# First attention of two layers: maxima, tables and the first scores in another order

## The chip, the cores and the metric

The kernel runs on one core of one Trainium2 chip. The metric is the device time of one execution in microseconds. Before the change the median of three runs is 3340.94 us (3340.58 to 3341.14).

The core has five engines with a queue each: TensorE (PE: products; its weight loads are shown as PEld), VectorE (DVE), ScalarE (ACT), GpSimd (POOL) and SyncE (SP, DMAs only). Semaphores are what they wait for each other by.

## The reference

Two model blocks of two layers each work on 512 tokens of width 1024, in float32. Only the first block is touched by the change. Cut to what matters, its layer is:

```python
h = rmsnorm(x, g_mix)
aq, ak, av, rq, rk, rv, rg, ga, gb = jnp.split(h @ w_in, SPLIT_POINTS, axis=-1)
aq, ak = rope_half(aq, pos), rope_half(ak, pos)
ya = sliding_window_sink_attention(aq, ak, av, sinks) @ w_a   # 8 heads, window 128
...                                                           # retention: yb
mixed = jax.nn.sigmoid(ga) * ya + jax.nn.sigmoid(gb) * yb
x = x + mixed @ w_out
x = x + jnp.square(jax.nn.relu(rmsnorm(x, g_mlp) @ w_up)) @ w_down
```

The attention takes the scores of 128 queries against up to 256 keys, adds a mask, takes the row maximum (with the sink), the exponential, the sum, divides, and multiplies by the values.

## The kernel before

**Tiling.** Activations lie transposed: 8 tiles of 128 features by 512 tokens. Each float32 product is split in three: high by high, high by low, low by high, each a PE product of 128x512 (`L526` to `L528`, or `L531`, `L532`, `L583` where a panel is taken row by row). Weights come as panels of 128x2048. SP loads a panel, ACT writes its high part (`L1257`), POOL the low part by a subtraction (`L357`, `L349`), and PE multiplies: a panel of two output tiles is 48 products, and half a tile is 12.

**The start of a layer of the first block.** `L667` are warm-up products on a constant tile, before the first panel (the program's first PE work). Then PE takes panel `q` (two head pairs) and panel `kv` (keys, values) on x times the gain, not yet normalised. ACT squares x, and DVE adds the squares (`L1961`). Behind four rows of `kv` PE adds over the features (`L660`, `token_sums`), ACT takes the root (`L1537`), DVE the inverse, and PE spreads it over the partitions (`L715`, `spread`). DVE multiplies the rotary tables by it (`L2283`), so that the rotation of q and k also normalises them. Then DVE scales x again and splits it into high and low parts (`L2010`, `L1939`, ACT's high part `L1277`) for the panels that need it normalised: panel `rq` is the fourth and the first of these.

**Rotation and first attention.** A rotation (`rope`) of one 128x512 tile is four DVE instructions: a shuffle and three elementwise ones (`L1944` to `L1950`). Head pairs 0 to 3 are rotated as 0, 1, 2, 3 and the keys as 4; layer 0 takes 0 before the scaling and 4, 1, 2, 3 behind it, layer 1 takes 0, 1, 4 before it and 2, 3 behind it. The attention then runs in 8 steps of two head pairs: PE's scores (`L746`; step 0 needs rotations 1 and 4, step 1 needs rotation 3, and each step the maxima of the one before, which free its bank), DVE's maxima (`L2055`, with the sink at `L2060`), ACT's exponentials (`L1311`), DVE's division, PE's transposes (`L754`), ACT's read of them (`L1321`), PE's outputs (`L766`) and their read (`L1326`). Between these, PE takes half tiles of other panels as fillers, 32 pieces in each layer.

**What sets the order.** It is written by hand, one list for each engine, and a wait names the mark of another engine's instruction. Each engine keeps its own order strictly. In layer 0 PE takes two filler pieces (one tile) ahead of scores 0, and ACT reads that tile and issues the second table's DMA before its first exponentials. The table of the second rotation (retention, `ROT`) may be loaded only once rotation 3 has used the first.

Of the kernel before, what the change touches and what calls it, by code (L numbers as in the profile page):

```python
# [191 lines left out]
SWAP_A = [r ^ 16 for r in range(32)]  # L192
# [34 lines left out]
def program(nc, stream, x_in, consts_in, rot_in, vec_in, wgate_in, pos_in, out, marks):  # L227
    ctx = ExitStack()
    with ctx:
# [282 lines left out]
        def _(pe):  # L512
# [150 lines left out]
            def start_clock(n):  # L663

                T.after("warm_tile", own=False)
                for _ in range(n):
                    pe.matmul(PS[:, 7, 0:2 * P], TMP[:, 3, 0:P], TMP[:, 3, 0:2 * P], start=True, stop=True)  # L667
# [300 lines left out]
                    marks[("panel", end - 2)] = ("up_full", base_t + 4 * groups - 2)  # L968
                marks[(t, l, "ffn_out")] = ("down_added", done)

            start_clock(5)
            for l in range(DEPTH):
                w, t = at_a(l), "a"
                h_ready = lambda k: (t, l, "h_lo", k)
# [6 lines left out]
                    run(keys, 4)  # L981
                token_sums(TMP[:, 2, :], 4, (t, l, "n1_acc", KD - 1), (t, l, "n1_ms"))
                bank_reader[4] = (t, l, "n1_root")
                run(keys, 2)
                spread(5, (t, l, "n1_inverse"), (t, l, "n1_spread"))
                bank_reader[5] = (t, l, "n1_scaled", KD - 1)
                for _ in keys:
# [19 lines left out]
                        yield from gemm_tiles(w["ga"] + p, KD, 2, XH, XL, h_ready, lambda m: (t, l, "ga", 2 * p + m), True)  # L1007
                    yield from tok_tiles(w["rv0"], h_ready, lambda m: (t, l, "rv", 0, m), True)

                attention(pairs_a(l), l, t, fillers(), 2 if l == 0 else 0)  # L1010
                for p in range(2):
                    if p:
                        gemm(w["wa"] + p, 4, 4, YH, YL, lambda k: (t, l, "ao_lo", k), lambda m: (t, l, "wa", 4 * p + m))
# [227 lines left out]
        def _(act):  # L1241
# [52 lines left out]
                e = 96 if eps == EPS else 97  # L1294
                A.done(act.activation(TMP[:, 3, :], sums, ACT.Sqrt, scale=1.0 / n, bias=ST[:, e:e + 1]), *name)

            def attention(pairs, l, t, fillers):
                steps = steps_of(pairs, t)
                last = len(steps) - 1

                def exponentials(i):
                    n, nk, c = len(steps[i]), steps[i][0]["nk"], 32 + 16 * (i % 2)
                    pr = probs(i, n * nk)
                    A.after((t, l, "negmax", i))
                    for u in range(n):
                        for v in range(2):
                            if u or v:
                                A.after()
                            e = pr[:, v, u * nk:(u + 1) * nk]
                            h = c + 2 * u + v  # L1310
                            A.done(act.activation(e, e, ACT.Exp, bias=ST[:, h + 4:h + 5],  # L1311
                                                  scale=-1.0, accum_out=ST[:, h + 8:h + 9]), t, l, "exp", i)
                    if steps[i][0]["sink"] is not None:
                        A.after()
                        sinks = ST[:, c + 12:c + 12 + 2 * n]
                        A.done(act.activation(sinks, sinks, ACT.Exp), t, l, "exp", i)

                def read_transposes(i):
                    w = len(steps[i]) * steps[i][0]["nk"]
                    A.after((t, l, "pt", i), (t, l, "o", i - 2) if i >= 2 else None)  # L1320
                    A.done(act.activation(probs_t(i, w), PS[:, 6:8, 0:w], ACT.Copy), t, l, "pt_read", i)  # L1321

                def read_outputs(i):
                    n = len(steps[i])
                    A.after((t, l, "o", i))
                    A.done(act.activation(steps[i][0]["o"](n), PS[:, 2, 0:n * P].rearrange("p (u s) -> p u s", u=n), ACT.Copy),  # L1326
                           t, l, "o_read", i)

                exponentials(0)
                exponentials(1)  # L1330
                run(fillers, tiles_in(t, -1))
                done = 0
                for i in range(last + 2):
                    if i <= last:
                        read_transposes(i)
                    if i:
                        read_outputs(i - 1)
                    if i + 2 <= last:
                        exponentials(i + 2)
                    if i <= last:  # L1340
                        run(fillers, tiles_in(t, i))
                    if i and steps[i - 1][0]["part"] == NB - 1:
                        for j in range(done, done + len(steps[i - 1])):
                            split_hi(YH[:, j, :], (AR[:, 14 + j, :] if t == "a" else AR[:, 8 + j, :]), [], (t, l, "ao_hi", j))
                        done += len(steps[i - 1])
                marks[(t, l, "pt_read")] = marks[(t, l, "pt_read", last)]
                for _ in fillers:
                    pass
# [244 lines left out]
            for l in range(DEPTH):  # L1593
# [45 lines left out]
                hi(w["rq"] + 2)  # L1639
                fill = filler_reads()  # L1640
                if l == 0:
                    run(fill)
                    const_dma(act, VEC[:, 1, :], vec_in[1], "vec1")
                A.after((t, l, "roped", 3))
                const_dma(act, ROT[:, :, :], rot_in[1], ("rot", l, 1))
                attention(pairs_a(l), l, t, fill)
                hi(w["wa"] + 1)
                if l + 1 < DEPTH:
                    A.after((t, l, "roped", 12))
# [280 lines left out]
        def _(dve):  # L1930
# [107 lines left out]
                        j = k - 1  # L2038
                        lo(XL[:, j, :], dst(j), XH[:, j, :], [hi_name(j)], lo_name(j), own=False)

            def attention(pairs, l, t, beside):
                steps = steps_of(pairs, t)
                last = len(steps) - 1

                def maxima(i):
                    n, nk, c = len(steps[i]), steps[i][0]["nk"], 32 + 16 * (i % 2)
                    pr = probs(i, n * nk)
                    sink = steps[i][0]["sink"]
                    V.after((t, l, "s", i), (t, l, "pt", i - 3) if i >= 3 else None, (t, l, "mask", steps[i][0]["part"]))
                    for u, U in enumerate(steps[i]):  # L2050
                        for v in range(2):
                            h = 2 * u + v
                            least = ST[:, 16 + sink + h:17 + sink + h] if sink is not None else -TAKEN
                            e = slice(u * nk, (u + 1) * nk)
                            V.done(dve.tensor_tensor_reduce(pr[:, v, e], U["mask"], PS[:, 4 + v, e], -(HD ** -0.5), least,  # L2055
                                                            ALU.add, ALU.min, ST[:, c + 4 + h:c + 5 + h]), t, l, "s_read", i)
                    marks[(t, l, "negmax", i)] = ("dve", V.n)
                    if sink is not None:
                        V.after()
                        V.done(dve.tensor_tensor(ST[:, c + 12:c + 12 + 2 * n], ST[:, c + 4:c + 4 + 2 * n],  # L2060
                                                 ST[:, 16 + sink:16 + sink + 2 * n], ALU.subtract), t, l, "negmax", i)

                def normalise(i):
                    n, nk, c = len(steps[i]), steps[i][0]["nk"], 32 + 16 * (i % 2)
                    pr = probs(i, n * nk)
                    V.after((t, l, "exp", i))
                    sums = ST[:, c + 8:c + 8 + 2 * n]
                    if steps[i][0]["sink"] is not None:
                        V.done(dve.tensor_tensor(sums, sums, ST[:, c + 12:c + 12 + 2 * n], ALU.add))
                        V.after()  # L2070
                    V.done(dve.reciprocal(ST[:, c:c + 2 * n], sums))
                    V.after()
                    if n == 1:
                        V.done(dve.tensor_tensor(pr, pr, ST[:, c:c + 2].unsqueeze(2).broadcast_to([P, 2, nk]), ALU.mult),
                               t, l, "p", i)
                    else:
                        for v in range(2):
                            e = pr[:, v, :].rearrange("p (u n) -> p u n", u=n)
                            V.done(dve.tensor_tensor(e, e, ST[:, c + v:c + 2 * n:2].unsqueeze(2).broadcast_to([P, n, nk]),
                                                     ALU.mult), t, l, "p", i)  # L2080

                maxima(0)
                maxima(1)
                for i in range(last + 1):
                    if t == "b":
                        run(beside, rounds(t, i))
                    normalise(i)
                    if i + 2 <= last:
                        maxima(i + 2)
                    if t == "a":  # L2090
                        run(beside, rounds(t, i))
                marks[(t, l, "s_read")], marks[(t, l, "negmax")] = marks[(t, l, "s_read", last)], marks[(t, l, "negmax", last)]
                for j in range(4):
                    lo(YL[:, j, :], AR[:, 14 + j, :] if t == "a" else AR[:, 8 + j, :], YH[:, j, :],
                       [(t, l, "ao_hi", j)], (t, l, "ao_lo", j))
# [175 lines left out]
            for l in range(DEPTH):  # L2271
# [13 lines left out]
                for j in early:  # L2285
                    rope(AR[:, j, :], SWAP_A, (t, l, "roped", j), [("read", t, l, "q", j)])
                scale_again(t, l, VA["g_mix"])
                for j in [j for j in (4, 1, 2, 3) if j not in early]:
                    rope(AR[:, j, :], SWAP_A, (t, l, "roped", j), [("read", t, l, "q", j)])

                def retention_ropes():
                    for j in range(8):
# [1 line left out]
                             YSCR[:, KD + 7, :])  # L2294
                        yield

                attention(pairs_a(l), l, t, retention_ropes())
                branch_gate(l, t)
                def per_chunk(c0):
                    return CT[:, c0:c0 + P].unsqueeze(1).broadcast_to([P, NB, P])  # L2300
# [257 lines left out]
```

How the kernel before makes its waits and increments, by code:

```python
    def after(self, *names, own=True):  # L205
        need = {}
        for name in names:
            if name is None or (name not in self.marks and not self.marks.get("complete")):
                continue
            who, n = self.marks[name]
            need[who] = max(need.get(who, 0), n)
        if own:
            need[self.name] = self.n
        for who, n in need.items():
            if n > 0:
                self.eng.wait_ge(self.sems[who], n)
# [65 lines left out]
        def const_dma(eng, dst, src, name):  # L283
            if n_consts[0]:
                eng.wait_ge(const_loaded, 16 * n_consts[0])
            eng.dma_start(dst, src).then_inc(const_loaded, 16)
            n_consts[0] += 1
            marks[name] = ("const", 16 * n_consts[0])
# [27 lines left out]
        @block.sync  # L317
# [6 lines left out]
            sp.dma_start(RAW[:, 1, :], stream[1:2, :, :].rearrange("o p n -> p (o n)")).then_inc(raw_full[1], 16)
            with sp.Fori(1, NPANELS // 2) as i:
                for s in range(2):
                    sp.wait_ge(lo_ready, 2 * i + s + 1)
                    sp.dma_start(RAW[:, s, :], stream[bass.ds(2 * i + s, 1), :, :].rearrange("o p n -> p (o n)"))\
                        .then_inc(raw_full[s], 16)
            for k in range(KD):
                sp.wait_ge(sems["act"], marks.get(("b", DEPTH - 1, "ln2_x", k), ("act", 1))[1])
                sp.dma_start(out.rearrange("(k p) s -> p k s", p=P)[:, k, :], X[:, k, :]).then_inc(stored, 16)
            sp.wait_ge(stored, 16 * KD)
```

## Time and profile before

| | us |
|---|---|
| median of the runs | 3340.94 |
| the profiled execution | 3339.35 |
| its span | 3337.5 |
| PE busy | 3301.5 (99%) |
| DVE busy | 1567.9 (47%) |
| ACT busy | 1370.2 (41%) |
| POOL busy | 1470.4 (44%) |
| waits of PE on the maxima before scores (`L746`) | 5.0, two times |
| waits of PE on ACT's first high part (`L531`) | 2.9, once |

Busy time is the time in which an engine has an instruction under way; since matmuls overlap, a busy PE may still run at half speed, which the busy share doesn't tell. The length of a product and the granted clock tell it. What PE waits for is named by the last semaphore that came.

### The profile page before, as it was taken

The numbers are of one execution on the slowest core, as the hardware profiler recorded it, in microseconds if no ns is written. First come the engines' busy times: TensorE is split into PE (matmuls) and PEld (weight loads), VectorE is DVE, ScalarE is ACT, GpSimd is POOL, SyncE is SP. The second block draws the span as 40 slices with busy tenths as digits, with TensorE's granted clock in tenths as the row PEclk, the third lists the DMA queues.
The fourth block names the chain that finished last, engine by engine and source line by source line (L and its number), as shares of the span: only waits on it lengthen the run. The fifth ranks groups of instructions, "written<-read, shape, count | busy, mean of one in ns | idle before, by whom it ended". The sixth has DMA issues, their size and how long they took to land. (4 is left out here: it accounts for less than half of the span.)

```text
span 3337.5 us, 45362 instructions
## 1 busy us (share of the span) xinstructions
PE 3301.5 (99%) x16670; PEld 2748.5 (82%) x16670; DVE 1567.9 (47%) x2488; ACT 1370.2 (41%) x1989; POOL 1470.4 (44%) x1102
## 2 busy tenths in 40 slices
PE   9999999999999999999999999999999999999998
PEld 7888888888788888888878888888887788888887
DVE  7523332226514442224973446544488625464445
ACT  5535332224635342223364453333343635443333
POOL 4433544445343444445433345445544233445453
PEclk9999999999999999999999999999999999999999
DMA  4222222222222322222211222222222121222221
GB/s 153 89 73 86 89 103 95 94 101 95 77 76 76 103 100 100 89 101 106 88 66 66 73 92 99 84 95 101 101 81 87 64 76 68 97 85 92 101 98 66
DMA packets 44014, 299.02 MB, mean 90 GB/s; under 512 B 4816, under 2 KB 5456, under 8 KB 8784
## 3 DMA queue, kind: packets, MB, share of 16 engines
q1 hardware_dynamic: 41696, 291.52, 24.5%
q10 hardware_dynamic: 2160, 5.33, 0.5%
q8 instruction: 107, 1.75, 0.2%
q14 instruction: 51, 0.42, 0.0%
HBM read 294.74 MB, written 2.10 MB: 89 GB/s over the span
## 5 line engine op out<-in xcount | busy, mean ns | idle before, releaser
L349 POOL TENSOR_TENSOR w_lo<-w_raw,w_hi 128x512 fp32r<-128x512 f32 x1024 | 1364.6, 1365 | 1778.2 <-ACT w_hi L1257 1778.2
L526 PE MATMUL ps<-x_hi,w_hi 128*128 128x512 f32 x2296 | 907.2, 395 | 3.1 <-DVE arena L2195 2.2
L528 PE MATMUL ps<-x_hi,w_lo 128*128 128x512 f32 x2296 | 894.8, 390 | 0.0
L527 PE MATMUL ps<-x_lo,w_hi 128*128 128x512 f32 x2296 | 894.1, 389 | 0.0
L1257 ACT ACTIVATE w_hi<-w_raw 128x1024 fp32r<-128x1024 f32 x516 | 515.9, 1049 | 463.0 <-PE ps L528 339.4
L526 PEld LDWEIGHTS ps<-x_hi,w_hi 128*128 128x128 f32 x2296 | 431.5, 188 | 100.3 <-issue 6.4
L528 PEld LDWEIGHTS ps<-x_hi,w_lo 128*128 128x128 f32 x2296 | 431.2, 188 | 91.2
L527 PEld LDWEIGHTS ps<-x_lo,w_hi 128*128 128x128 f32 x2296 | 431.6, 188 | 89.0 <-issue 2.2
L526 PE MATMUL ps<-y_hi,w_hi 128*128 128x512 f32 x1056 | 411.9, 390 | 2.2 <-issue 1.9
L528 PE MATMUL ps<-y_hi,w_lo 128*128 128x512 f32 x1056 | 410.9, 389 | 0.0
L527 PE MATMUL ps<-y_lo,w_hi 128*128 128x512 f32 x1056 | 410.8, 389 | 0.0
L2236 DVE TENSOR_TENSOR x<-x,ps 128x512 f32<-128x512 f32 x272 | 182.2, 684 | 255.5 <-PE ps L528 255.3
L2195 DVE SCALAR_TENSOR_TENSOR arena<-ps,vec,arena 128x511 f32<-128x511 f32 (+1 forms) x176 | 131.5, 749 | 300.4 <-ACT arena L1467 290.1
L526 PEld LDWEIGHTS ps<-y_hi,w_hi 128*128 128x128 f32 x1056 | 198.2, 188 | 45.1 <-issue 4.2
L527 PEld LDWEIGHTS ps<-y_lo,w_hi 128*128 128x128 f32 x1056 | 198.2, 188 | 41.5 <-issue 0.5
L528 PEld LDWEIGHTS ps<-y_hi,w_lo 128*128 128x128 f32 x1056 | 198.2, 188 | 41.3
L632 PE MATMUL ps<-w_hi,x_hi 128*128 128x256 f32 x768 | 222.2, 289 | 1.2 <-POOL w_lo L349 1.2
L633 PE MATMUL ps<-w_hi,x_lo 128*128 128x256 f32 x768 | 217.1, 283 | 0.0
L634 PE MATMUL ps<-w_lo,x_hi 128*128 128x256 f32 x768 | 217.1, 283 | 0.0
L1273 ACT ACTIVATE arena<-ps 128x512 f32<-128x512 f32 x136 | 81.3, 598 | 315.8 <-PE ps L528 240.6
L1467 ACT ACTIVATE arena<-ps,vec 128x512 f32<-128x512 f32 x88 | 68.4, 779 | 277.4 <-PE ps L528 277.4
L2206 DVE SCALAR_TENSOR_TENSOR arena<-ps,tmp 128x512 f32<-128x512 f32 x64 | 44.0, 691 | 238.5 <-PE ps L528 224.9
(269 smaller groups left out, 4178.7 us busy)
## 6 DMA issues: line engine op xcount, KB each, us to landing
w_raw<-stream SPq DMA_DIRECT2D x274, 1024.0 KB, 4.8
x<-x_t SPq DMA_DIRECT2D x4, 512.0 KB, 8.1
rotary<-rot ACTq DMA_DIRECT2D x4, 512.0 KB, 4.0
y_t<-x SPq DMA_DIRECT2D x8, 256.0 KB, 2.1
ct<-consts ACTq DMA_DIRECT2D x2, 770.0 KB, 4.4
arena<-pos ACTq DMA_DIRECT2D x2, 256.0 KB, 2.6
w_gate<-w_gate_in ACTq DMA_DIRECT2D x2, 256.0 KB, 2.8
vec<-vectors ACTq DMA_DIRECT2D x4, 116.0 KB, 2.0
```

The lines of the kernel that those rows point to most:

```text
L349: ins = nc.gpsimd.tensor_tensor(low(c)[:, o:o + S], RAW[:, c % 2, o:o + S], high(c)[:, o:o + S].bitcast(F32), ALU.subtract)
L526: pe.matmul(ps, wh, xh, start=(k == 0), stop=False)
L527: pe.matmul(ps, wh, xl, start=False, stop=False)
L528: return pe.matmul(ps, wl, xh, start=False, stop=last)
L632: pe.matmul(ps, xh, wh, start=(k == 0), stop=False)
L633: pe.matmul(ps, xl, wh, start=False, stop=False)
L634: mm = pe.matmul(ps, xh, wl, start=False, stop=(k == KD - 1))
L1257: act.activation(wh[:, o:o + 2 * S], RAW[:, s, o:o + 2 * S], ACT.Copy)\
L1273: A.done(act.activation(dst, bank_of(*name), func, **kw), *(("read",) + name))
L1467: act.activation(AR[:, j, :], PS[:, j, :], ACT.Identity, scale=VEC[:, l % 2, bass.ds(tap, 1)], bias=VEC[:, l % 2, bass.ds(bias, 1)]).then_ ...
L2195: ins = dve.scalar_tensor_tensor(AR[:, j, tap:S], PS[:, j, 0:n], wv, AR[:, j, tap:S], ALU.mult, ALU.add)
L2236: dve.tensor_tensor(X[:, m, :], X[:, m, :], PS[:, 4 + m % 4, :], ALU.add).then_inc(down_added, 1)
```

## The change

It moves instructions and adds three warm-up products. In words:

- PE warms up with eight products in place of five.
- The spread of the inverse root comes behind one more row of the `kv` panel, not two.
- In layer 0, PE asks for scores 0 directly behind the fourth panel (`rq`); the tile that ran ahead is now among the later fillers.
- ACT issues the DMA of the second rotary table behind exponentials 0, and in layer 0 reads one tile later.
- DVE takes maxima 0 before rotations 2 and 3, and maxima 1 behind them, in both layers.

```diff
-            start_clock(5)
+            start_clock(8)
...
-                run(keys, 2)
+                run(keys)
                 spread(5, (t, l, "n1_inverse"), (t, l, "n1_spread"))
...
-                attention(pairs_a(l), l, t, fillers(), 2 if l == 0 else 0)
+                attention(pairs_a(l), l, t, fillers())
...  ACT
                 exponentials(0)
+                for _ in behind_first:
+                    pass
                 exponentials(1)
...
                 if l == 0:
-                    run(fill)
                     const_dma(act, VEC[:, 1, :], vec_in[1], "vec1")
-                A.after((t, l, "roped", 3))
-                const_dma(act, ROT[:, :, :], rot_in[1], ("rot", l, 1))
-                attention(pairs_a(l), l, t, fill)
+
+                def second_table():
+                    A.after((t, l, "roped", 3))
+                    const_dma(act, ROT[:, :, :], rot_in[1], ("rot", l, 1))
+                    yield
+
+                attention(pairs_a(l), l, t, fill, second_table())
...  DVE
                 maxima(0)
+                for _ in behind_first:
+                    pass
                 maxima(1)
...
-                for j in [j for j in (4, 1, 2, 3) if j not in early]:
+                for j in [j for j in (4, 1) if j not in early]:
                     rope(AR[:, j, :], SWAP_A, (t, l, "roped", j), [("read", t, l, "q", j)])
+
+                def last_ropes():
+                    for j in (2, 3):
+                        rope(AR[:, j, :], SWAP_A, (t, l, "roped", j), [("read", t, l, "q", j)])
+                        yield
...
-                attention(pairs_a(l), l, t, retention_ropes())
+                attention(pairs_a(l), l, t, retention_ropes(), last_ropes())
```

On PE, in layer 0, at the end of the fourth panel (`L532` and `L583` are its last row; `arena` under `L746` holds the rotated queries and keys), before:

```order
162 L531 MATMUL ps<-x_hi,w_hi 128x512
163 L532 MATMUL ps<-x_hi,w_lo 128x512
164 L583 MATMUL ps<-x_lo,w_hi 128x512 x2
165 L526 MATMUL ps<-x_hi,w_hi 128x512
166 L527 MATMUL ps<-x_lo,w_hi 128x512
```

and now:

```order
162 L531 MATMUL ps<-x_hi,w_hi 128x512
163 L532 MATMUL ps<-x_hi,w_lo 128x512
164 L583 MATMUL ps<-x_lo,w_hi 128x512 x2
165 L746 MATMUL ps<-arena 128x128 x4
166 L526 MATMUL ps<-x_hi,w_hi 128x512
```

Scores 0 stood behind 24 filler products, at row 189, and stand ahead of them now. Scores 1 follow behind 12 products in both.

On DVE, in layer 0, behind rotations 4 and 1 (a rotation is the shuffle and three rows; `ISA` are the maxima, the second row of each pair reading out the minimum), before:

```order
40 L1944 STREAM_SHUFFLE tmp<-arena 128x512
41 L1946 TENSOR_TENSOR tmp<-tmp,rotary 128x512
42 L1948 TENSOR_TENSOR arena<-arena,rotary 128x512
43 L1950 TENSOR_TENSOR arena<-arena,tmp 128x512
44 L2055 ISA tmp,stats<-ct,ps,stats 128x128
45 L2055 ISA stats 128x1
```

and now:

```order
42 L2060 ISA tmp,stats<-ct,ps,stats 128x128
43 L2060 ISA stats 128x1
44 L2065 TENSOR_TENSOR stats<-stats 128x4
45 L1949 STREAM_SHUFFLE tmp<-arena 128x512
46 L1951 TENSOR_TENSOR tmp<-tmp,rotary 128x512
47 L1953 TENSOR_TENSOR arena<-arena,rotary 128x512
```

Rows 36 to 43 were rotations 2 and 3, with maxima 0 behind them in rows 44 to 52; now maxima 0 are rows 36 to 44 and the rotations rows 45 to 52. The same swap stands in layer 1. (Lines behind the diff's additions are five higher in the changed kernel.)

On ACT, in layer 0, around the first exponentials (`L1311`), before:

```order
22 L1257 ACTIVATE w_hi<-w_raw 128x1024 x2
23 L1273 ACTIVATE arena<-ps 128x512
24 L287 DMA vec<-vectors 128x232
25 L287 DMA rotary<-rot 128x1024
26 L1311 ACT_TABLE_LOAD
27 L1311 ACTIVATE tmp,stats<-tmp,stats 128x128 x4
```

and now:

```order
22 L1257 ACTIVATE w_hi<-w_raw 128x1024 x2
23 L287 DMA vec<-vectors 128x232
24 L1311 ACT_TABLE_LOAD
25 L1311 ACTIVATE tmp,stats<-tmp,stats 128x128 x4
26 L1316 ACTIVATE stats<-stats 128x4
27 L287 DMA rotary<-rot 128x1024
```

The read of the first filler tile (`L1273`) has gone behind exponentials 1, and the DMA of the table stands between exponentials 0 and 1.

## Rows read from the trace of the kernel before

**Rows 1.** The page, busy time, share and instructions of each engine.
```profile
PE 3301.5 (99%) x16670; PEld 2748.5 (82%) x16670; DVE 1567.9 (47%) x2488; ACT 1370.2 (41%) x1989; POOL 1470.4 (44%) x1102
```

**Rows 2.** Timeline of the start: begin, length, engine, line, tiles, [idle before].
```profile
1.35 4.64 PE L667 MATMUL ps<-tmp 128*128 128x256 f32 x10 [1.35 <-DVE tmp L1935]
...
8.91 0.77 PE L531 MATMUL ps<-x_hi,w_hi 128*128 128x512 f32 x1 [2.92 <-ACT x_hi L1566]
...
14.15 0.39 PE L531 MATMUL ps<-x_hi,w_hi 128*128 128x512 f32 x1
```

**Rows 3.** Timeline, sums of squares, token sums and spread of layer 0.
```profile
19.84 8.35 DVE L1961 TENSOR_TENSOR tmp<-tmp,scratch 128x512 f32<-128x512 f32 x6
...
28.25 1.05 PE L660 MATMUL ps<-ct,tmp 128*128 128x1 f32 x8 [0.29 <-DVE tmp L1961]
...
32.02 1.05 PE L715 MATMUL ps<-ct,stats 128*128 128x128 f32 x8
```

**Rows 4.** Timeline of ACT, the read of the keys and the first split.
```profile
35.65 1.29 ACT L1273 ACTIVATE arena<-ps 128x512 f32<-128x512 f32 x2 [6.04 <-PE ps L583]
...
38.73 1.14 ACT L1277 ACTIVATE x_hi<-tmp 128x512 fp32r<-128x512 f32 x2
```

**Rows 5.** Timeline of DVE, layer 0, splits, rotations 1 to 3, maxima 0.
```profile
39.38 1.68 DVE L1939 TENSOR_TENSOR x_lo<-tmp,x_hi 128x512 fp32r<-128x512 f32 x1 [0.38 <-ACT x_hi L1277]
...
58.75 0.69 DVE L1950 TENSOR_TENSOR arena<-arena,tmp 128x512 f32<-128x512 f32 x1
...
62.06 1.66 DVE L1948 TENSOR_TENSOR arena<-arena,rotary 128x512 f32<-128x512 f32 x1
...
67.87 0.69 DVE L1950 TENSOR_TENSOR arena<-arena,tmp 128x512 f32<-128x512 f32 x1
...
69.94 0.16 DVE L2060 TENSOR_TENSOR stats<-stats 128x4 f32<-128x4 f32 x1
```

**Rows 6.** Timeline of PE, layer 0, fourth panel's end to scores 2.
```profile
57.45 0.61 PE L583 MATMUL ps<-x_lo,w_hi 128*128 128x512 f32 x2
...
63.43 0.71 PE L746 MATMUL ps<-arena 64*128 64x128 f32 x8
...
66.70 0.39 PE L528 MATMUL ps<-x_hi,w_lo 128*128 128x512 f32 x1
70.05 0.81 PE L746 MATMUL ps<-arena 64*128 64x128 f32 x8 [2.95 <-DVE stats L2055]
...
73.72 1.13 PE L746 MATMUL ps<-arena 64*128 64x256 f32 x8
```

**Rows 7.** Timeline of POOL, its run behind the fourth panel in each layer.
```profile
60.18 6.38 POOL L349 TENSOR_TENSOR w_lo<-w_raw,w_hi 128x512 fp32r<-128x512 f32 x4 [5.06 <-ACT w_hi L1257]
...
829.47 5.62 POOL L349 TENSOR_TENSOR w_lo<-w_raw,w_hi 128x512 fp32r<-128x512 f32 x4 [3.26 <-ACT w_hi L1257]
```

**Rows 8.** Timeline of PE, layer 1, scores 0, 1 and 2.
```profile
827.27 0.71 PE L746 MATMUL ps<-arena 64*128 64x128 f32 x8
832.99 1.12 PE L746 MATMUL ps<-arena 64*128 64x128 f32 x8 [2.06 <-DVE stats L2055]
838.24 1.14 PE L746 MATMUL ps<-arena 64*128 64x256 f32 x8
```

**Rows 9.** Timeline of DVE, layer 1, rotation 2's start, 3's end, maxima 0.
```profile
823.49 0.75 DVE L1944 STREAM_SHUFFLE tmp<-arena 128x512 f32<-128x512 f32 x1
...
829.84 1.67 DVE L1950 TENSOR_TENSOR arena<-arena,tmp 128x512 f32<-128x512 f32 x1
...
832.88 1.00 DVE L2060 TENSOR_TENSOR stats<-stats 128x4 f32<-128x4 f32 x1
```

**Rows 10.** Stretch, its length, busy time by engine, granted PE clock, DMA.
```profile
833.00:837.00 4.00, 4.00 (x16) 3.17 (x17) 2.87 (x13) 3.09 (x13) 2.09 (x2) 0.57 0.50 156
```

**Rows 11.** Timeline of PE, the `wa` panel's start in layers 0 and 1.
```profile
173.56 0.47 PE L531 MATMUL ps<-y_hi,w_hi 128*128 128x512 f32 x1 [1.77 <-ACT arena L1326]
...
942.81 0.47 PE L531 MATMUL ps<-y_hi,w_hi 128*128 128x512 f32 x1 [0.84 <-ACT scratch L1273]
```

More of the change, by code:

```diff
@@ L1295, in root, with attention @@
                 A.done(act.activation(TMP[:, 3, :], sums, ACT.Sqrt, scale=1.0 / n, bias=ST[:, e:e + 1]), *name)
-            def attention(pairs, l, t, fillers):
+            def attention(pairs, l, t, fillers, behind_first=iter(())):
                 steps = steps_of(pairs, t)
@@ L2039, in norm, with attention @@
                         lo(XL[:, j, :], dst(j), XH[:, j, :], [hi_name(j)], lo_name(j), own=False)
-            def attention(pairs, l, t, beside):
+            def attention(pairs, l, t, beside, behind_first=iter(())):
                 steps = steps_of(pairs, t)
```

## The prediction

> **What bounds the kernel now.** I read the page's busy shares first, then the timeline of TensorE (PE) around each place that the diff touches, then the other engines at the same times, then the granted clock. PE is busy 3301.5 us of the 3337.5 [rows 1], so every microsecond in which PE waits or runs at half speed is a microsecond of the end, and a microsecond on another engine counts only if PE waits for it. The question is therefore where PE waits in the changed stretches, and what ends each wait.
>
> Three stretches matter. **The start**: warm-up products until 5.99, an idle 2.92 us, then the first panel from 8.91. The reader is to see that 128x512 products last 0.63 to 0.77 us here and 0.39 from 14.15 on [rows 2]: twelve products from 8.91 to 14.15 take 5.24 us, where twelve at the later pace of 0.227 us from start to start take 2.7. That is TensorE at 1.2 and then at 2.4 GHz. **First attention of layer 0**: PE sits idle 2.95 us before the second scores, at 70.05, behind VectorE's (DVE's) rotations and first maxima [rows 5, 6]. **The same place in layer 1**: 2.06 us idle before 832.99 [rows 8, 9].
>
> **Warm-up of eight products in place of five.** Five took 4.64 us, so three more take at most 2.8 and end at about 8.8, before the first panel's product at 8.91, which waits for data: they cost nothing. They may let that panel run at full speed, 2.5 us sooner. But the next thing that PE needs is the sum of squares: DVE adds until 28.19 (19.84 plus 8.35), and PE starts the token sums at 28.25, having waited 0.29 us for it already [rows 3]. DVE's chain doesn't depend on PE there. So the 2.5 us turn into a wait at the token sums of about 2.7 us, and the gain is 0. The bounds are -2.5 (carried through) and +1.6 to +1.7 (the new wait brings the clock down, see below); I take 0, since the row shows the next wait standing.
>
> **Spread one row sooner.** Its eight instructions move ahead of one row of six products, 1.4 us. DVE then scales the tables and rotates head pair 0 that much sooner. In layer 0 its next link is the first split: ScalarE (ACT) makes the high part at 38.73, right behind its weight halves, which wait for PE's keys read at 35.65 [rows 4], and DVE's first low part follows at 39.38 [rows 5]. The keys panel ends at the same time, since the spread only changed places inside it. In layer 1 rotation 4 needs the same read. Cost 0, bounds -1.4 and 0 per layer; 0, for the same reason as above.
>
> **Layer 0: the order around the first scores.** In the changed kernel PE asks for scores 0 at 57.90, right behind the fourth panel [rows 6] (57.45 plus two products), but they need rotation 1, which ends at 59.44 [rows 5]. With 0.15 us for the hand-over they run 59.6 to 60.3. DVE, free at 59.44, waits for them, then takes the maxima: 1.5 us in the calm (68.56 to 70.10) [rows 5], 2.4 us while GpSimd (POOL) subtracts (831.51 to 833.88) [rows 9]. POOL is at work from 60.18 to 66.56 [rows 7], so 2.4: until 62.7. Only now come rotations 2 and 3. One elementwise step of a rotation takes 0.69 us in the calm and 1.66 beside POOL (58.75 and 62.06) [rows 5], the shuffle 0.75 either way, so a rotation takes 3.0 or 5.9 us. Rotation 2: shuffle to 63.5, two slow steps to 66.9, one fast to 67.6; rotation 3 to 70.7; scores 1 start at 70.85. Before they started at 70.05. So removing the maxima from behind the rotations gains nothing: DVE has idled 0.9 us for the scores and pays for the maxima ahead of the rotations instead of behind them.
>
> Meanwhile PE has lost its cover. Before, it computed a whole tile (24 products) before scores 0, from 57.90 to 63.43 or 5.5 us, and half a tile behind them. Now only the half is left: PE idles 57.9 to 59.6, works to 63.1, and idles about 7.7 us until 70.85. The tile is still owed. Loss: 0.8 + 5.5 = 6.3 us. Bounds: +3.5 (all rotations calm, below) and +7.2 (one more slow step).
>
> The tile comes back at the end of attention, where the fillers of layer 0 had run out: PE idled 1.77 us before the `wa` panel. Layer 1, which never ran ahead, idled 0.84 there [rows 11]. Layer 0 now has layer 1's order: -0.9.
>
> **Layer 1.** Rotations 0, 1 and 4 stand early, so PE starts scores 0 at 827.27 in both kernels. Before, DVE went straight from the splits into rotation 2 at 823.49 [rows 9]. Now it waits from there to 828.0 with nothing to do: 4.5 us thrown away. Maxima in the calm to 829.5; POOL works from 829.47 to 835.09 [rows 7], so rotation 2 takes 5.9, to 835.4, and rotation 3 takes 3.0, to 838.4; scores 1 at 838.6 against 832.99 [rows 8]. Loss: 5.6 us; bounds +2.8 (calm) and +6.6.
>
> **The clock.** The 2.06 us idle of layer 1 was followed by a granted clock of 0.57 over 833 to 837 [rows 10], part of it at 1.2 GHz; scores 1 and the half tile behind them took 5.25 us there (832.99 to 838.24) [rows 8] and 3.67 in layer 0 (70.05 to 73.72) [rows 6], whose 2.95 us idle left the clock up. So one drop cost 1.6 us, and the start paid 2.5; a wait of 2 to 3 us may or may not bring one. I take it that 7.7 us do, in both layers, for 2.1 us each, the middle of the two prices. Layer 1 paid 1.6 already: +2.1 and +0.5. Bounds for both together: -1.6 (no drop at all) and +3.4.
>
> The page "TensorE: Matmul & The Clock Gate" of the Trainium skill (Part 1, the two states) says that an idle array falls back to 1.2 GHz and must work for a while before it is let up again. By that rule both long waits drop the clock, as I take it; by the layer 0 row alone, where a wait left the clock up, the sum would be 3.7 us less (2.1 + 1.6). This case shows one wait of each kind.
>
> **ACT and the rest.** The rotary table's DMA moves behind exponentials 0 and still waits for rotation 3; exponentials 1 need maxima 1, later still, so nothing queues behind it that was ready. One read of layer 0 moves behind the exponentials; its bank isn't asked for until two tiles later. Both 0. The exponential table load now hides in a wait: 0, since p 0 is needed only after the half tile.
>
> **Sum.** 0 + 0 + 6.3 - 0.9 + 5.6 + 2.6 = +13.6 us. The profiled execution took 3339.35 us, 1.85 outside its span: 3352.95. The median of the runs is 3340.94, 1.6 higher: 3354.5 us.
>
> **Rivals.**
> A. The new wait at the token sums, 2.7 us, drops the clock as the 2.06 did: the keys panel ends 1.6 later and the whole chain behind it. 3356.1. For: [rows 10]; against: layer 0's 2.95. Chance 0.25.
> B. The clock stays up through the long waits, or rises at once: +13.6 - 2.6 - 1.6 = +9.4, 3350.3. Against it is [rows 10]. Chance 0.12.
> C. The other side: the rotations run clear of POOL. Then scores 1 come at 60.3 + 1.5 + 6.1 + 0.15 = 68.05 in layer 0 (-2.0 + 5.5 = +3.5) and at 829.5 + 6.25 = 835.75 in layer 1 (+2.8); with -0.9, no drop in layer 1 (-1.6) and the warm start carried through (-2.5) that is +1.3: 3342.2, no change. It decides whether POOL's run, which follows the end of the fourth panel by about 2.3 us, still meets the rotations. Nothing moves it away, so 0.06.
> D. The change does what its words say: the scores sooner, the maxima off the path, the warm start kept; that would be -2.5 at the start and -1.5 per layer, 3335.4. For it stands only that PE's wait ended on the maxima; against it, that PE would have to need scores 1 later, not sooner. 0.03, and not all of that reaches beyond 0.2%.
>
> The forecast itself has 0.48; 0.06 is left for waits that I don't see, mostly longer. A measurement here tells 0.2%, 6.7 us, from no change: slower means above 3347.6. Slower 0.90 (forecast, A, B and most of the unseen), same 0.07 (C and a little), faster 0.03. The range of 3349.5 to 3358.5 takes in B and A and the bounds on the clock; it leaves out C, D, and the upper bounds of everything at once.
>
> **What the changed profile would show.** Right: products of 0.39 us from 8.9 on, and a PE wait of 2 to 3 us before the token sums at about 28.2; scores 0 at 59.6; scores 1 near 70.9 and 838.6, each behind 7 to 8 us of PE idle ended by DVE's rotation (no longer by the maxima); DVE idle 4.5 us before the layer 1 maxima; 0.5 granted somewhere in these waits and behind them; 0.8 us idle before `wa` in both layers. Wrong: scores 1 before 69 or 836 (rotations calm), token sums well before 28.2 (the start gains), or a PE that waits for something else behind scores 1.

## The result, and the profile after

The changed kernel takes 3353.73 us (median of five runs, 3352.71 to 3354.64) against 3341.08 for the kernel before on the same chip: 12.65 us slower, ratio 1.0036 with a 95% interval of 1.0024 to 1.0048 (the two medians alone give 1.0038). Forecast were 3354.5 us and slower. The profiled execution took 3352.71 us, 13.36 over the profiled one of before, and its span is 3350.9 us, 13.4 over. One later run of the kernel before, of 3649.38 us at a granted clock of 0.849, is left out of every comparison here.

PE's waits over the whole span, longest first: who waited for whom, total, times, longest.

```profile
PE ps L746 <- DVE arena L1955: 15.3, 3, 7.0
...
PE ps L531 <- ACT scratch L1273: 1.7, 2, 0.8
PE ps L660 <- DVE tmp L1966: 1.4, 1, 1.4
...
PE ps L531 <- ACT x_hi L1568: 1.0, 1, 1.0
```

The scores (`L746`) now wait for the last step of a rotation, three times and 15.3 us in all, where they waited twice and for the maxima before [rows 6, 8]. Timeline of PE at the start (begin, length, engine, line, tiles, idle before):

```profile
1.36 6.40 PE L667 MATMUL ps<-tmp 128*128 128x256 f32 x16 [1.36 <-DVE tmp L1940]
8.75 0.47 PE L531 MATMUL ps<-x_hi,w_hi 128*128 128x512 f32 x1 [0.99 <-ACT x_hi L1568]
...
10.24 0.73 PE L583 MATMUL ps<-x_lo,w_hi 128*128 128x512 f32 x2 [0.34 <-DVE x_lo L2002]
...
10.81 0.40 PE L531 MATMUL ps<-x_hi,w_hi 128*128 128x512 f32 x1
...
12.51 0.39 PE L531 MATMUL ps<-x_hi,w_hi 128*128 128x512 f32 x1
```

Answering to [rows 2]: the warm-up ends at 7.76, the first panel runs at full speed from its first product, and its rows follow each other by 1.70 us (10.81 to 12.51) where six products take 1.36, because DVE's low parts are late. At the token sums, PE waits 1.44 us (the third row of waits above) and starts them at 28.09, against 28.25 [rows 3].

Timeline of PE in layer 0, scores 0, 1 and 2, and in layer 1 the same:

```profile
59.44 0.81 PE L746 MATMUL ps<-arena 64*128 64x128 f32 x8 [1.55 <-DVE arena L1955]
69.91 1.31 PE L746 MATMUL ps<-arena 64*128 64x128 f32 x8 [6.72 <-DVE arena L1955]
75.92 1.13 PE L746 MATMUL ps<-arena 64*128 64x256 f32 x8
...
834.18 0.72 PE L746 MATMUL ps<-arena 64*128 64x128 f32 x8
844.84 1.31 PE L746 MATMUL ps<-arena 64*128 64x128 f32 x8 [6.99 <-DVE arena L1955]
850.78 1.14 PE L746 MATMUL ps<-arena 64*128 64x256 f32 x8
```

Layer 0: scores 1 start where they started before (70.05, [rows 6]), but with a tile less computed. Layer 1: 10.66 us from scores 0 to scores 1, where it was 5.72 [rows 8]. From scores 1 to scores 2 PE takes 6.01 and 5.94 us for what took 3.67 in layer 0 before. The reason stands in the table by stretch (length, busy time by engine, granted clock, DMA share, GB/s):

```profile
63.00:70.00 7.00, 0.28 (x2) 0.12 (x1) 6.44 (x9) 1.78 (x9) 2.46 (x2) 0.88 0.41 150
70.00:73.00 3.00, 3.00 (x12) 2.42 (x13) 1.56 (x11) 0.34 (x2) 0.00 (x0) 0.50 0.56 175
...
845.00:849.00 4.00, 4.00 (x15) 3.20 (x16) 2.43 (x13) 1.35 (x6) 0.00 (x0) 0.50 0.84 342
```

The clock falls to 0.50, 1.2 GHz, during the idle and stays there for the first products behind it. (At the start I had read the clock from the length of the products alone. In the profile of before, the granted clock reads 1.00 from 9 to 12 us, where the products last 0.63 us; in the profiles of two kernels below with the same start (half a tile ahead in layer 1, and the waits covered) it reads 0.52 and 0.50 there, with products of the same length. For the start, go by the length.) What DVE does meanwhile, layer 0:

```profile
60.28 0.35 DVE L2060 CUSTOM_DVE_ANT_0 tmp<-ct,ps,stats 128x128 f32<-128x128 f32 x1 [0.99 <-DMA vec<-vectors]
...
61.48 1.09 DVE L2065 TENSOR_TENSOR stats<-stats 128x4 f32<-128x4 f32 x1
...
64.37 1.64 DVE L1953 TENSOR_TENSOR arena<-arena,rotary 128x512 f32<-128x512 f32 x1
66.04 0.69 DVE L1955 TENSOR_TENSOR arena<-arena,tmp 128x512 f32<-128x512 f32 x1
...
69.08 0.69 DVE L1955 TENSOR_TENSOR arena<-arena,tmp 128x512 f32<-128x512 f32 x1
```

and layer 1:

```profile
834.95 0.35 DVE L2060 CUSTOM_DVE_ANT_0 tmp<-ct,ps,stats 128x128 f32<-128x128 f32 x1 [4.68 <-PE ps L746]
...
838.26 1.64 DVE L1953 TENSOR_TENSOR arena<-arena,rotary 128x512 f32<-128x512 f32 x1
839.93 1.64 DVE L1955 TENSOR_TENSOR arena<-arena,tmp 128x512 f32<-128x512 f32 x1
```

The reader sees DVE idle 0.99 and 4.68 us for the first scores, the maxima ahead of the rotations, and rotation 3 ending only at 69.77 in layer 0. (The releaser of the first row is named as a DMA; that row waits for scores 0 too, which end at 60.25, just ahead of it.) The wait ahead of the `wa` panel, answering to [rows 11], is 0.84 in both layers:

```profile
180.50 0.47 PE L531 MATMUL ps<-y_hi,w_hi 128*128 128x512 f32 x1 [0.84 <-ACT scratch L1273]
...
955.36 0.47 PE L531 MATMUL ps<-y_hi,w_hi 128*128 128x512 f32 x1 [0.84 <-ACT scratch L1273]
```

By these two rows the difference is +6.94 us at layer 0's `wa` (173.56 before) and +12.55 at layer 1's (942.81), so 6.94 and 5.61 for the layers; the last 0.8 us came later, where nothing was changed. From layer 1's `wa` to the end of the span it is 2394.7 us before and 2395.5 now.

### The profile page after: what moved, and what is told of

Its sections match the earlier page's. It is cut to its first block and busy times, and to the rows that moved or that the text cites. A ratio compares the mean times of both kernels' runs of the same rounds, so it can differ in the third digit from the quotient of the medians.

```text
span 3350.9 us, 45373 instructions
## 1 busy us (share of the span) xinstructions
PE 3305.2 (99%) x16676; PEld 2750.9 (82%) x16676; DVE 1562.2 (47%) x2488; ACT 1370.4 (41%) x1989; POOL 1467.3 (44%) x1102
## 5 line engine op out<-in xcount | busy, mean ns | idle before, releaser
L1273 ACT ACTIVATE arena<-ps 128x512 f32<-128x512 f32 x136 | 81.4, 598 | 318.7 <-PE ps L528 243.7
```

Of the source, the lines that this page charges most:

```text
L1273: A.done(act.activation(dst, bank_of(*name), func, **kw), *(("read",) + name))
```

## The experiments

Times are medians of 5 to 11 runs. The experiments ran on three chips, each with the kernel before beside them, 21 to 30 times:

| chip | kernels | kernel before, median |
|---|---|---|
| first | DVE's order undone; the tile ahead again; the start alone; layer 1's swap alone | 3341.91 |
| second | the idle filled; POOL later; half a tile ahead in layer 1; the same with POOL later | 3341.09 |
| third | the changed kernel again; with the old start; the start alone, filled; the waits covered | 3342.09 |

So each kernel is compared by its distance from the kernel before on its own chip. The changed kernel's own distance is 12.65 us as first measured and 11.1 when it was repeated on the third chip, so a part taken as a difference to it is uncertain by 1.5 us. The single runs of the kernel before lie between 3339.3 and 3345.5 us. Of those executions only one has a profile; profiles of the other kernels differ by drops of the clock that come in some and not in others, which is the likely reason for the spread.

**DVE's order undone.** Changed kernel, with

```diff
-                attention(pairs_a(l), l, t, retention_ropes(), last_ropes())
+                for _ in last_ropes():
+                    pass
+                attention(pairs_a(l), l, t, retention_ropes())
```

> The changed kernel with one part undone: DVE takes rotations 2 and 3 ahead of maxima 0 again, in both layers. My theory (layer 0 pays for the tile that no longer runs ahead, layer 1 for the maxima between the rotations): layer 1 is back at 5.7 us from scores 0 to scores 1; layer 0 keeps its loss, scores 1 still at about 70.0 with some 8 us of PE idle around scores 0, so 6.9 us over the kernel before, 3348.0 us. Rival (DVE's order is the whole cost): 3341. Rival (the tile is the whole cost in both): 3353.

3347.29 us, ratio to before 1.0017 (1.0008 to 1.0027): 5.4 us over the kernel before, 6.9 expected. Its scores 0 and 1 in layer 0, and scores 1 in layer 1:

```profile
61.13 0.80 PE L746 MATMUL ps<-arena 64*128 64x128 f32 x8 [1.53 <-DVE arena L1955]
71.54 1.32 PE L746 MATMUL ps<-arena 64*128 64x128 f32 x8 [6.62 <-DVE stats L2060]
...
841.97 1.10 PE L746 MATMUL ps<-arena 64*128 64x128 f32 x8 [2.05 <-DVE stats L2060]
```

Layer 1 is back at its 2.05 us, layer 0 keeps a wait of 6.62: scores 1 follow scores 0 by 10.41 us, 10.47 in the changed kernel. So the swap on DVE is layer 1's loss, and costs layer 0 nothing that the missing tile doesn't cost anyway.

**The tile ahead again, DVE's order kept.** Changed kernel, with

```diff
-                attention(pairs_a(l), l, t, fillers())
+                attention(pairs_a(l), l, t, fillers(), 2 if l == 0 else 0)
...
                 if l == 0:
+                    run(fill)
                     const_dma(act, VEC[:, 1, :], vec_in[1], "vec1")
```

> The changed kernel with the other part undone: in layer 0 PE takes the tile ahead of scores 0 again and ACT reads it; DVE's maxima stay between the rotations. My theory: DVE now waits for scores 0 until about 64 in layer 0, scores 1 come at about 72.5 (2.5 later than before), with 6 us of PE idle that still bring the clock down (2.3); layer 1 keeps its 5.6. Sum 10.4 over the kernel before, 3351.5 us. Rival (the tile covers DVE, layer 0 is free again): 3346.7. Rival (the tile was all): 3341.

3350.89 us, ratio 1.0027 (1.0017 to 1.0037): 9.0 over the kernel before, 10.4 expected.

```profile
64.92 0.71 PE L746 MATMUL ps<-arena 64*128 64x128 f32 x8
73.28 1.32 PE L746 MATMUL ps<-arena 64*128 64x128 f32 x8 [4.70 <-DVE arena L1956]
...
843.02 1.32 PE L746 MATMUL ps<-arena 64*128 64x128 f32 x8 [7.00 <-DVE arena L1956]
```

With the tile, scores 1 come 8.36 us behind scores 0 (6.62 before, [rows 6]): DVE's swap costs layer 0 too as soon as it has the tile. The two parts of the change overlap there. PE's idle is 4.70 us, where I had expected 6.

**The start alone.** Kernel before, with

```diff
-            start_clock(5)
+            start_clock(8)
...
-                run(keys, 2)
+                run(keys)
```

> The kernel before with the start alone changed: eight warm-up products and the spread one row sooner. My theory: PE runs the first panel at full speed and then waits 1.4 us at the token sums for DVE's squares, which start at 28.1 as before; 3341 us, within 0.5 of before. Rival (the warm start carries through): 2.5 less, 3338.5. Rival (the wait costs the clock): 1.7 more, 3342.7.

3343.78 us, ratio 1.0002 (0.9993 to 1.0012): no gain, and 1.9 us above before within the noise. In the profile the clock's rival happened (the second line is a stretch, as above):

```profile
28.14 1.05 PE L660 MATMUL ps<-ct,tmp 128*128 128x1 f32 x8 [1.47 <-DVE tmp L1961]
29.00:33.00 4.00, 4.00 (x18) 3.55 (x18) 0.67 (x3) 0.27 (x1) 1.45 (x2) 0.65 0.25 78
...
64.89 0.72 PE L746 MATMUL ps<-arena 64*128 64x128 f32 x8
```

The token sums start on time behind 1.47 us of idle, the granted clock is 0.65 over the stretch from 29 to 33 us, and scores 0 are 1.46 late (63.43 in [rows 6]). Layer 0's wait of 2.98 us, which the kernel before has too, is also followed by a drop here, where the profile of before shows none. Eight profiles have this start with the wait open (the changed kernel twice, and six of the variants); four of them show the loss, four (the changed kernel's both) don't. The old start isn't free of it: in two profiles below with five warm-up products, the changed kernel with the old start and half a tile ahead in layer 1, the first panel came up to full speed sooner than the 14.15 of [rows 2] (products of 0.40 us from 12.60 and from 11.99 on), PE waited 1.12 and 1.38 us at the token sums, and the clock was 0.57 and 0.58 over 29 to 33 us. So whether this drop comes is partly chance with either start.

**The start alone, its wait filled.** As the run before, with

```diff
+                if l == 0:
+                    keep_clock(7, 1)
                 token_sums(TMP[:, 2, :], 4, (t, l, "n1_acc", KD - 1), (t, l, "n1_ms"))
```

> The start alone changed (eight warm-up products, spread a row sooner), and two products of constants (128x256) ahead of the token sums in layer 0, inside the new wait of 1.5 us. My theory: the new wait costs nothing by itself but sometimes brings the clock down for 3.4 us; with 0.9 us of it filled the drop goes, scores 0 of layer 0 at 63.3 as before: 3341.1, level with the kernel before and 1.9 below the start alone (3343.8). Rival (the start's 1.9 is chance): 3343 as without.

3341.83 us against 3342.09, ratio 1.0000 (0.9991 to 1.0009); scores 0 at 63.37. As expected in size, but the step from 1.0002 lies inside the noise: that the filling did it is not shown by the times, and the one profile can't show it.

**Layer 1's swap alone.** Changed kernel with layer 0 of before: the tile ahead as above, and

```diff
-                attention(pairs_a(l), l, t, retention_ropes(), last_ropes())
+                if l == 0:
+                    for _ in last_ropes():
+                        pass
+                attention(pairs_a(l), l, t, retention_ropes(), last_ropes() if l else iter(()))
```

> The changed kernel with layer 0 as before (tile ahead, rotations 2 and 3 ahead of maxima 0); layer 1 keeps the maxima between the rotations. My theory: layer 1 alone costs 5.6 us (4.9 of late rotation 3, 0.7 of clock), 3346.7 us; layer 0's scores 1 at 70 as before. Rival (layer 1's loss is a consequence of layer 0's shift in time or of its clock): 3341 to 3343.

3346.67 us, ratio 1.0017 (1.0008 to 1.0027): 4.8 over the kernel before, 5.6 expected.

```profile
69.97 1.31 PE L746 MATMUL ps<-arena 64*128 64x128 f32 x8 [2.97 <-DVE stats L2061]
...
840.72 1.32 PE L746 MATMUL ps<-arena 64*128 64x128 f32 x8 [7.00 <-DVE arena L1956]
```

Layer 1 loses by itself. Layer 0's wait of 2.97 is the old one, yet the clock fell in it this time (1.31 for the scores, 0.81 in [rows 6]).

**The idle filled.** Changed kernel, with

```diff
                 run(fillers)
+                if t == "a":
+                    keep_clock(6, 6)
                 scores(1)
```

> The changed kernel with twelve more products of constants by constants (128x256, their result is used by nothing) ahead of scores 1 in both layers, inside the idle time of 6.7 and 7.0 us. They measure what the clock costs. My theory: the clock stays up, scores 1 to scores 2 take 3.7 us in place of 6.0 and 5.9, so 4.5 us less than the changed kernel, 3349.2 us; scores 1 start where they did. Rival (the clock drop is not from the idle, or costs nothing): 3353.7. Rival (the products are longer than the idle): more than 3353.7.

3350.66 us, ratio 1.0025 (1.0015 to 1.0036): 9.6 over the kernel before, so 3.1 less than the changed kernel as first measured (1.5 less than in its repeat); 4.5 expected.

```profile
64.71 5.34 PE L674 MATMUL ps<-ct 128*128 128x256 f32 x24
71.59 0.80 PE L746 MATMUL ps<-arena 64*128 64x128 f32 x8 [1.54 <-DVE arena L1957]
...
844.22 0.80 PE L746 MATMUL ps<-arena 64*128 64x128 f32 x8 [1.83 <-DVE arena L1957]
849.48 1.14 PE L746 MATMUL ps<-arena 64*128 64x256 f32 x8
```

In layer 0 scores 2 followed 3.70 us behind scores 1 (6.01 without): the clock cost 2.3. In layer 1 the 1.83 us left open were followed by a drop: 5.26. Neither moved scores 1 away from scores 0 (10.49 and 10.67), so the rest of the loss is the wait itself.

**POOL later.** Changed kernel, with `hi(w["rq"] + 2)` taken from ahead of the attention and put behind the wait for rotation 3:

```diff
                     A.after((t, l, "roped", 3))
                     const_dma(act, ROT[:, :, :], rot_in[1], ("rot", l, 1))
+                    hi(w["rq"] + 2)
                     yield
```

> The changed kernel with the high halves of the sixth weight panel, which start POOL's subtractions, moved behind rotation 3 on ACT, in both layers. My theory (half of DVE's slow steps are POOL's doing): the minimum with the sink falls from 1.09 to 0.16 in layer 0, rotation 2 takes 3.0 in both, so scores 1 come 2.0 sooner in layer 0 and 2.3 in layer 1: 3349.4 us. Rival (DVE's slow steps don't come from POOL): 3353.7. Rival (the panel is then late for PE): a wait on the low half behind scores 2, and more than 3353.7.

3349.04 us, ratio 1.0022 (1.0012 to 1.0032): 8.0 over the kernel before, so 4.7 less than the changed kernel as first measured (3.2 less than in its repeat); 4.3 expected.

```profile
61.58 0.17 DVE L2065 TENSOR_TENSOR stats<-stats 128x4 f32<-128x4 f32 x1
...
63.38 0.69 DVE L1953 TENSOR_TENSOR arena<-arena,rotary 128x512 f32<-128x512 f32 x1
```

and on PE, scores 0 and 1 of layer 0:

```profile
59.54 0.81 PE L746 MATMUL ps<-arena 64*128 64x128 f32 x8 [1.54 <-DVE arena L1955]
67.97 1.32 PE L746 MATMUL ps<-arena 64*128 64x128 f32 x8 [4.66 <-DVE arena L1955]
```

Every slow step is gone (1.09 and 1.64 us above), and scores 1 follow scores 0 by 8.43 and 8.35 us, 2.04 and 2.31 sooner. The edit moves ACT's high halves too, but in the changed kernel these end at 60.88, ahead of the slow steps (61.48 to 66.01), while POOL is at work from 60.00 to 65.46. So POOL's subtractions are what makes DVE's two-input steps more than twice as long. The page "GPSIMD Engine Reference" of the Trainium skill (1. Specifications) says that POOL shares its SBUF interfaces with VectorE and contends with instructions with two SBUF inputs; these runs agree, and the maxima, with one SBUF input beside PSUM, kept their 0.35 us beside POOL.

**The changed kernel again, and with the old start.** The second is the changed kernel with `start_clock(5)` and `run(keys, 2)`.

> The changed kernel as it is, beside the others on one chip, so that the parts can be subtracted from it there. My theory: 12.6 over the kernel before as first measured (3353.7 there). Rival (the difference depends on where the clock's drops fall, and here the kernel before has more of them): 10 to 11 over it.

> The changed kernel with the start of before (five warm-up products, spread behind two rows). My theory: layers 0 and 1 keep their 6.9 and 5.6, the start gives nothing or takes up to 1.9 by the clock; within -1.9 and 0 of the changed kernel. Rival (the warm start does bring something): 0.3 to 2.5 above the changed kernel.

3353.22 and 3354.55 us: 11.1 and 12.5 over the kernel before on that chip, ratios 1.0035 (1.0021 to 1.0049) and 1.0036 (1.0022 to 1.0049). The changed kernel's time repeats; its distance of 11.1 is nearer the rival's 10 to 11 than my 12.6, since the kernel before took 1.0 us more here. The kernel with the old start lies 1.3 us above the changed one, inside the rival's 0.3 to 2.5 and outside my range. But the runs overlap (3352.45 to 3355.05 and 3352.54 to 3354.78), and its profile has the drop at the token sums that both profiles of the changed kernel lack, with scores 0 at 61.14 and not 59.44. So a gain of the warm start of about 1 us is neither shown nor ruled out.

**The other way round: half a tile ahead in layer 1.** Kernel before, with

```diff
-                attention(pairs_a(l), l, t, fillers(), 2 if l == 0 else 0)
+                attention(pairs_a(l), l, t, fillers(), 2 if l == 0 else 1)
```

> The kernel before with half a tile taken ahead of scores 0 in layer 1 too (12 products that stood later). My theory, the other way round: cover is what counts. Scores 0 at 830.0, DVE not ready for them before 831.6, scores 1 at about 833.5 without idle, no drop of the clock: 2.1 of wait and 1.6 of clock gained, 0.9 lost at the end of attention, 3338.1 us. Rival (the fillers are missed at the end, for as much): 3341.

3341.85 us, ratio 0.9998 (0.9988 to 1.0007): my 3 us of gain didn't come.

```profile
836.76 0.72 PE L746 MATMUL ps<-arena 64*128 64x128 f32 x8
...
943.93 0.76 PE L531 MATMUL ps<-y_hi,w_hi 128*128 128x512 f32 x1 [2.65 <-ACT scratch L1273]
```

Scores 1 have no wait any more, 3.59 us behind scores 0. But the end of attention waits 2.65 us (0.84 before, 1.77 expected), and products of 0.76 us show the clock down behind it. The wait had moved, with its clock.

**The same with POOL later in layer 1.** There, `hi(w["rq"] + 2)` goes behind rotation 3 in layer 1 alone.

> As the run with half a tile ahead in layer 1, and there the sixth panel's high halves behind rotation 3 on ACT. My theory: rotation 3 and the maxima end 1.8 us sooner, but PE is no longer waiting for them, so this adds at most 0.5 us of gain: 3338 us. Rival (DVE still bounds scores 1): 3336.5. Rival (exponentials 0 wait behind the weight halves, transposes 0 late): 3340.

3338.05 us, ratio 0.9995 (0.9985 to 1.0004). Scores 1 and the wait ahead of `wa` are as in the run above:

```profile
941.00 0.47 PE L531 MATMUL ps<-y_hi,w_hi 128*128 128x512 f32 x1 [2.74 <-ACT scratch L1273]
```

The 3.8 us between the two medians weren't expected (0.5 at most). The two profiles are 4.4 us apart, and these are drops of the clock: the one above has them behind the token sums, behind layer 0's scores 1 and behind this `wa` panel's start (granted clock 0.58, 0.57 and 0.61 over 29 to 33, 73 to 77 and 944 to 948 us), this one has 1.00 in all three. The first two make 2.98 us at layer 0's `wa`, in code that is the same. Whether POOL's place has any part in it stays open.

**The waits covered.** The same, with products of constants in what idle is left:

```diff
                 run(fillers)
+                if t == "a" and l == 0:
+                    keep_clock(6, 3)
                 scores(1)
...
                 attention(pairs_a(l), l, t, fillers(), 2 if l == 0 else 1)
+                keep_clock(6, 1 + l)
```

> The kernel before, with layer 1's half tile ahead and its sixth panel behind rotation 3 (the run at 3338.05), and products of constants inside the waits that are left: six ahead of scores 1 in layer 0 (2.6 of 2.95 us), two and four ahead of the wa panel (0.9 of 1.8, 1.7 of 2.7 us). My theory: they cost nothing and hold the clock up, so that the time lies at the low end of that run's, 3337.2 us. Rival (they lengthen the path, since the waits end on semaphores that come during them): 3339 to 3340.

3337.96 us against 3342.09, ratio 0.9988 (0.9979 to 0.9997): the one kernel that is faster than before beyond its interval, by 4.1 us. It holds no part of the change.

```profile
66.66 2.75 PE L674 MATMUL ps<-ct 128*128 128x256 f32 x12
69.78 0.83 PE L746 MATMUL ps<-arena 64*128 64x128 f32 x8 [0.37 <-DVE stats L2061]
...
940.49 0.47 PE L531 MATMUL ps<-y_hi,w_hi 128*128 128x512 f32 x1 [0.73 <-ACT scratch L1276]
```

The products cost the path nothing that can be seen. Against the run above its median is the same (3338.05; 4.1 and 3.0 below the kernel before on their chips); what is less is the spread, 3337.4 to 3339.8 against 3337.2 to 3342.9.

## Why the prediction was right

- **Start: 0, right in size, with a wrong part.** The new wait was 1.4 us, not 2.7: I had the first panel bound by PE at full speed, and it is bound by DVE's low parts, 1.70 us a row. The wait of 2 to 3 us that I gave as a sign therefore didn't show, though the next wait took the whole gain, as forecast. Rival A, the clock at the token sums, happened in four of the eight profiles with this start and in neither of the changed kernel; that it stayed away there is luck.
- **Spread: 0, right.** DVE scaled the tables from 31.57 (33.12 before) and then waited 1.76 us for the same split, which began at 39.20.
- **Layer 0: +6.3 - 0.9 + 2.1 forecast, 7.5; 6.94 measured.** Scores 1 came at 69.91, not 70.85: rotation 2 met POOL in one whole step and not two, since POOL itself finished sooner, at 65.46, with fewer DVE steps against it. The tile was 5.5 us, the end of attention gave back 0.93, the clock cost 2.34. PE's wait was 6.72 us, not 7.7.
- **Layer 1: +5.6 + 0.5, 6.1; 5.61 measured.** 4.94 of wait and 0.69 of clock. DVE's idle was 4.68 us, 4.5 forecast; one rotation step was half slow where I had taken it whole.
- **The later 0.8 us** was in no step. In the second block the transposes wait 0.6 us for DVE once where they didn't; why is open. It isn't the change's: in the profile of the changed kernel's repeat this wait is missing, and from layer 1's `wa` to the end it takes 2394.8 us, as before (2394.7).

The sum was 13.6, from the profiled execution; between the profiled executions it measured 13.36, between medians 12.65, and 11.1 in the repeat. The layers came to 1.05 us less than forecast (0.56 and 0.49), and in the profile the later 0.8 us made up for most of that, by luck. By the experiments, the kernel with the swap undone is 5.4 us over before and the one with layer 0's order given back 4.8; from the changed kernel's 11.1 to 12.65 they take away 5.7 to 7.3 (layer 1, forecast 6.1) and 6.4 to 7.9 (layer 0, forecast 7.5). So both terms have the sign and the size forecast. Rival C is ruled out by the slow steps of DVE, D by the time, and B by the granted clock of 0.50 and by the filled idle.

## What to carry to other kernels

When an engine waits behind a list of work, reordering that list helps only if its own input is there: before moving a step ahead on one engine, look up when its input comes and what the engine will do until then. Work that a busy engine runs ahead of a wait is cover, and moving it behind the wait costs its full length while the wait still ends at the same time (5.5 us here), though the count of instructions stays the same. And price a new idle on TensorE twice, once as itself and once as half-speed products behind it.

## What the hardware showed that I had not expected

- Waits of 1.1 to 3 us brought the clock down in some executions and not in others, in the same code. Layer 0's wait of 2.95 to 2.98 us was followed by a drop in three of six profiles, and the waits of 1.1 to 1.5 us at the token sums in six of ten. Layer 1's 2.06 us was followed by one in all four that have it. Ahead of layer 1's `wa`, 2.65 us was and 2.74 us wasn't. Each drop cost 1.5 to 2.9 us. The unfilled waits of 4.66 to 7.00 us ahead of scores 1 brought it down in every profile taken.
- The kernel before spreads over 6 us, likely for this reason (not shown, as it has one profile); its five first runs, within 0.6 us of each other, didn't show it.
- The slowing between DVE and POOL is mutual: in layer 0 POOL's four subtractions took 6.38 us beside three whole slow steps of rotations (1.65 to 1.67 us each) and 5.46 in the changed kernel beside one (1.64) and two shorter ones.
